# Expert gate and up weights in 1024-column pieces, and new PSUM banks for a task

## The reference

```
logits = (h @ w_router[i]).astype(F32)
top_v, top_i = lax.top_k(logits, TOP_K)                # TOP_K = 2 of N_EXP = 8
top_w = jax.nn.softmax(top_v, axis=-1)
for e in range(N_EXP):
    y = y + gates[..., e:e + 1] * swiglu(h, w_ex_gate[i, e], w_ex_up[i, e], w_ex_down[i, e])
# swiglu(h, wg, wu, wd) = (silu(h @ wg) * (h @ wu)) @ wd;  wg, wu: 1024 x 1408, wd: 1408 x 1024
```

## Time and profile before

| | us |
|---|---|
| median of 3 runs | 1520.3 |
| all runs | 1519.97, 1520.3, 1526.85 |
| span of the profiled execution (its time outside the span is not given) | 1521.1 |
| PE busy | 1484.1 |
| weight loads (PEld) busy | 1308.1 |
| DVE busy | 933.3 |
| ACT busy | 779.7 |

### The profile page before, as it was taken

The page is one execution under the profiler, slowest core; times in us unless marked ns, Lnnn a source line. Parts: engine busy times, 40 slices in busy tenths (PEclk is TensorE's granted clock), DMA queues, the critical chain, the costliest instruction groups (busy, mean ns, idle before and its releaser), DMA issues.

```text
span 1521.1 us, 22063 instructions
## 1 busy us (share of the span) xinstructions
PE 1484.1 (98%) x8722; PEld 1308.1 (86%) x8722; DVE 933.3 (61%) x1062; ACT 779.7 (51%) x889; POOL 53.7 (4%) x54
## 2 busy tenths in 40 slices
PE   7999999999999999999999999999999999999997
PEld 5788969699899999997889697998888888888875
DVE  4542265555554254346513655556998898988988
ACT  4443254543432242235333544535778778787875
POOL 0100000000000000001000000000000000000002
PEclk9999999999999999999999999999999999999999
DMA  9854265567752454265333554535999999999994
GB/s 327 269 171 160 97 222 166 167 213 234 259 161 93 149 135 121 91 221 171 122 118 111 167 167 139 167 115 184 332 369 392 381 381 374 377 389 380 374 383 160
DMA packets 236196, 342.50 MB, mean 225 GB/s; under 512 B 8661, under 2 KB 157054, under 8 KB 235854
## 3 DMA queue, kind: packets, MB, share of 16 engines
q1 hardware_dynamic: 227552, 313.32, 60.5%
q0 software_dynamic: 6496, 24.69, 4.4%
q10 hardware_dynamic: 2062, 3.24, 0.6%
HBM read 325.74 MB, written 15.47 MB: 224 GB/s over the span
## 4 chain that ended last, share of the span: by engine, by line
PE 90%; DVE 4%; DMA 2%; ACT 2%; SPq 1%; issue 1%; DVEq 0%; ACTq 0%
PE ps L701 26%; PE ps L703 26%; PE ps L702 25%; PE ps L718 2%; PE ps L943 2%; DMA raw<-in_w_ada_dram 1%; DVE wlo L2229 1%; PE ps L977 1%; SPq L476 1%; PE ps L961 1%; PE ps L728 1%; PE ps L1182 1%; DMA raw<-in_w_in_dram 1%; PE ps L799 1%; ACT whi L1647 1%
## 5 line engine op out<-in xcount | busy, mean ns | idle before, releaser
L701 PE MATMUL ps<-hhi,whi 128*128 128x384 f32 x824 | 276.6, 336 | 0.3 <-DVE hidlo L2326 0.3
L703 PE MATMUL ps<-hhi,wlo 128*128 128x384 f32 x824 | 275.3, 334 | 0.0
L702 PE MATMUL ps<-hlo,whi 128*128 128x384 f32 x824 | 275.3, 334 | 0.0
L1840 DVE TENSOR_TENSOR wlo<-raw,whi 128x2048 fp32r<-128x2048 f32 x65 | 148.7, 2289 | 179.2 <-ACT whi L1381 167.7
L2229 DVE TENSOR_TENSOR wlo<-raw,whi 128x2048 fp32r<-128x2048 f32 (+1 forms) x81 | 179.0, 2227 | 27.5 <-ACT whi L1647 26.9
L1647 ACT ACTIVATE whi<-raw 128x2048 fp32r<-128x2048 f32 (+1 forms) x81 | 150.5, 1868 | 49.9 <-PE ps L703 48.3
L2229 DVE TENSOR_TENSOR wlo<-mraw,whi 128x2048 fp32r<-128x2048 f32 (+2 forms) x81 | 160.7, 1992 | 14.8 <-ACT whi L1647 14.4
L701 PE MATMUL ps<-whi,xgh 128*128 128x512 f32 (+1 forms) x432 | 164.0, 380 | 3.5 <-DVE wlo L2229 2.0
L1647 ACT ACTIVATE whi<-mraw 128x2048 fp32r<-128x2048 f32 (+2 forms) x81 | 136.1, 1681 | 49.0 <-PE ps L703 48.9
L703 PE MATMUL ps<-whi,xgl 128*128 128x512 f32 (+1 forms) x432 | 160.9, 372 | 0.0
L702 PE MATMUL ps<-wlo,xgh 128*128 128x512 f32 (+1 forms) x432 | 160.5, 372 | 0.0
(11 more groups left out here) (352 smaller groups left out, 2495.3 us busy)
## 6 DMA issues: line engine op xcount, KB each, us to landing
raw<-in_w_ada_dram SPq DMA_DIRECT2D x62, 512.0 KB, 5.6
raw<-in_w_ex_up_dram SPq DMA_DIRECT2D x27, 1024.0 KB, 7.3
raw<-in_w_ex_down_dram SPq DMA_DIRECT2D x27, 1024.0 KB, 5.3
raw<-in_w_gate_dram SPq DMA_DIRECT2D x48, 512.0 KB, 4.6
raw<-in_w_in_dram SPq DMA_DIRECT2D x44, 512.0 KB, 6.0
raw<-in_w_ex_gate_dram SPq DMA_DIRECT2D x18, 1024.0 KB, 7.7
mraw<-in_w_ex_gate_dram SPq DMA_DIRECT2D x18, 1024.0 KB, 8.4
mraw<-in_w_ex_down_dram SPq DMA_DIRECT2D x18, 1024.0 KB, 8.8
```

Of the source, the lines that this page charges most:

```text
L701: pe.matmul(out, s[0], m[0], start=first, stop=False, **kw)
L702: pe.matmul(out, s[0], m[1], start=False, stop=False, **kw)
L703: return pe.matmul(out, s[1], m[0], start=False, stop=last, **kw)
L1840: dve.tensor_tensor(wlo[:, n % RING, :], raw[:, n % RING, :], whi[:, n % RING, :].bitcast(F32), ALU.subtract).then_inc(lo_done, 1)
```

## The change

A gate or up slot is now either wide, two channel tiles of 1024 columns (slots 0 to 3 gate, 4 to 7 up), or rest, four channel tiles of 384 columns (8 and 9 gate, 10 and 11 up). Slot sizes, their number and the six and three buffers stay. A wide slot's DMA reads runs of 4 KB, where all 512-column pieces had runs of 2 KB. One Silu and one product cover 1024 columns. The Silus stand in ACT's iterations 4 and 10, the products in DVE's 8 and 12, the turned products behind slots 8, 9 and 13, and `ehh` and `ehl` in iterations 9, 10 and 14. Banks: gate 0 and 1, up 2 and 3, rest 4 and 5, down output 6 and 7; turned products in 0, 1 and 4. `evalu` has memory of its own. The waits for `xg_ready` stand at slots 0 and 2 instead of 0 and 1.

```diff
-E_USED = [4 * CHUNKS[s // 4] for s in range(E_GU)] + [len(f) * D for f in E_DOWN]
+E_USED = [2 * WIDE] * (2 * E_WIDE) + [4 * CHUNKS[2]] * 4 + [len(f) * D for f in E_DOWN]
+TURNED = (0, 1, 4)
...
-                if s < E_GU:
-                    c, which, kh = s // 4, s % 4 // 2, s % 2
+                if s < 2 * E_WIDE:
+                    which, kp = divmod(s, E_WIDE)
+                    d = mraw[j][:, 0:E_USED[s]].rearrange("p (k c) -> p k c", k=2)
+                    src = w[which][:, 2 * kp:2 * kp + 2, 0:WIDE]
+                elif s < E_GU:
+                    which, kh = divmod(s - 2 * E_WIDE, 2)
                     d = mraw[j][:, 0:E_USED[s]].rearrange("p (k c) -> p k c", k=4)
-                    src = w[which][:, 4 * kh:4 * kh + 4, 512 * c:512 * c + CHUNKS[c]]
+                    src = w[which][:, 4 * kh:4 * kh + 4, WIDE:F_U]
...
-                    if s < 2:
-                        pe.wait_ge(xg_ready, 2 * q + s + 1)
+                    if s in (0, 2):
+                        pe.wait_ge(xg_ready, 2 * q + s // 2 + 1)
...
-                    if s % 4 == 0 and c != 1:
-                        pe.wait_ge(val_done, q * 3 + (3 if c == 0 else 4))
...
+                        for k in range(2):
+                            kk = 2 * kp + k
+                            for c in range(2):
+                                mm = mm3(ps[:, 2 * which + c, :], [y[:, kk, :] for y in (xgh, xgl)],
+                                         [y[:, k, 512 * c:512 * c + 512] for y in w], kk == 0, kk == KD - 1)
...
-                    if s in (5, 9):
-                        hidden_turned(s // 4 - 1, q)
+                    if s in (8, 9):
+                        hidden_turned(s - 8, q)
                     if s == 4 and more:
+                        pe.wait_ge(yv_ev, q + 1)
                         slots_of(q + 2)
...
+                        if more:
+                            pe.wait_ge(idx_ready, q + 1)
...
-                    if s in (2, 6, 10):
+                    if s == E_WIDE:
...
+                        act.activation(esil[:, :], ps[:, 0:2, :].rearrange("p a c -> p (a c)"), ACT.Silu).then_inc(esil_done, 1)
...
-                    if s in (4, 8, 12):
+                    if s == 2 * E_WIDE:
...
+                        dve.tensor_tensor(evalu[:, :], esil[:, :], ps[:, 2:4, :].rearrange("p a c -> p (a c)"), ALU.mult
+                                          ).then_inc(val_done, 1)
```

More of the change, by code:

```diff
@@ L270, in prefix_step_kernel @@
         assert rowx_at + 8 * BLK * N_EXP <= oraw_at
-        assert 5632 + 8 * KF * P <= 3 * 4 * 4 * T and 4 * SLOT * (MRAW - RING) + 12 * D <= top[0] - shared
+        assert 5632 + 8 * KF * P <= 3 * 4 * 4 * T and 4 * SLOT * (MRAW - RING) + 12 * D + 4 * WIDE <= top[0] - shared
         ssum = at("ssum", 2 * T, olo_at + 3072, shape=[2, T])
@@ L1177, in hidden_turned @@
             def hidden_turned(c, q):
-                pe.wait_ge(val_done, q * 3 + (c + 4))
-                pe.wait_ge(ehid_done, q * 3 + (c + 2))
+                pe.wait_ge(val_done, q * 2 + (4 if c == 2 else 3))
+                x = 512 * (c % 2)
                 for i in range(CHUNKS[c] // P):
-                    mm = pe.transpose(ps[:, 6 + c % 2, i * P:(i + 1) * P], evalu[:, i * P:(i + 1) * P], ident)
+                    mm = pe.transpose(ps[:, TURNED[c], i * P:(i + 1) * P], evalu[:, x + i * P:x + (i + 1) * P], ident)
                 mm.then_inc(ht_done, 1)
@@ L1187, in expert_task @@
                 for s in range(E_GU):
-                    c, which, kh = s // 4, s % 4 // 2, s % 2
-                    if s < 2:
-                        pe.wait_ge(xg_ready, 2 * q + s + 1)
+                    if s in (0, 2):
+                        pe.wait_ge(xg_ready, 2 * q + s // 2 + 1)
                     pe.wait_ge(lo_done, q * E_UNIT + split_count(n0 + s + 1))
-                    if s % 4 == 0 and c != 1:
-                        pe.wait_ge(val_done, q * 3 + (3 if c == 0 else 4))
[L1194 to L1198, removed]
+                    if s < 2 * E_WIDE:
+                        which, kp = divmod(s, E_WIDE)
+                        w = [x[:, s % RING, 0:E_USED[s]].rearrange("p (k c) -> p k c", k=2) for x in (whi, wlo)]
+                        for k in range(2):
[3 more added lines that the diff above has]
+                                         [y[:, k, 512 * c:512 * c + 512] for y in w], kk == 0, kk == KD - 1)
+                    else:
+                        which, kh = divmod(s - 2 * E_WIDE, 2)
+                        w = [x[:, s % RING, 0:E_USED[s]].rearrange("p (k c) -> p k c", k=4) for x in (whi, wlo)]
+                        for k in range(4):
+                            kk = 4 * kh + k
+                            mm = mm3(ps[:, 4 + which, 0:CHUNKS[2]], [y[:, kk, :] for y in (xgh, xgl)],
+                                     [y[:, k, :] for y in w], kk == 0, kk == KD - 1)
                     mm.then_inc(mm_done, 1)
-                    if s in (5, 9):
-                        hidden_turned(s // 4 - 1, q)
+                    if s in (8, 9):
+                        hidden_turned(s - 8, q)
                     if s == 4 and more:
+                        pe.wait_ge(yv_ev, q + 1)
                         slots_of(q + 2)
@@ L1214, in expert_task @@
                         for m in range(2):
-                            mm = mm3(ps[:, 4 + m, :], [y[:, kf, :] for y in (ehh, ehl)],
+                            mm = mm3(ps[:, 6 + m, :], [y[:, kf, :] for y in (ehh, ehl)],
                                      [y[:, c, m * 512:(m + 1) * 512] for y in w], kf == 0, kf == KF - 1)
@@ L1659, in expert_task @@
                         expert_hi(s + 2, q)
-                    if s in (2, 6, 10):
-                        c = s // 4
+                    if s == E_WIDE:
                         act.wait_ge(mm_done, q * E_UNIT + (n0 + s))
[L1663 to L1666, removed]
+                        act.wait_ge(val_done, q * 2 + 2)
+                        act.activation(esil[:, :], ps[:, 0:2, :].rearrange("p a c -> p (a c)"), ACT.Silu).then_inc(esil_done, 1)
+                    if s == 10:
+                        act.wait_ge(mm_done, q * E_UNIT + (n0 + s))
+                        act.wait_ge(val_done, q * 2 + 3)
+                        act.activation(esil[:, 0:CHUNKS[2]], ps[:, 4, 0:CHUNKS[2]], ACT.Silu).then_inc(esil_done, 1)
+                    if s in (9, 10, 14):
+                        c = min(s - 9, 2)
                         act.wait_ge(ht_done, q * 3 + (c + 1))
@@ L1670, in expert_task @@
                         act.activation(ehh[:, 4 * c:4 * c + CHUNKS[c] // P, :].rearrange("p k c -> p (k c)"),
-                                       ps[:, 6 + c % 2, 0:CHUNKS[c]], copy).then_inc(ehh_done, 1)
+                                       ps[:, TURNED[c], 0:CHUNKS[c]], copy).then_inc(ehh_done, 1)
                     if s == 13 and more:
@@ L1675, in expert_task @@
                         act.wait_ge(choice_tr, 1)
-                        act.activation(gat[:, :, :].rearrange("p b c -> p (b c)"), ps[:, 7, 0:T], copy).then_inc(choice_ready, 1)
+                        act.activation(gat[:, :, :].rearrange("p b c -> p (b c)"), ps[:, 5, 0:T], copy).then_inc(choice_ready, 1)
                         act.wait_ge(row_ready, 1)
@@ L1685, in expert_task @@
                 act.wait_ge(yd_out, q * 16 + 32)
-                act.activation(ysb[:, 0:512], ps[:, 4, :], copy).then_inc(ya_ev, 1)
+                act.activation(ysb[:, 0:512], ps[:, 6, :], copy).then_inc(ya_ev, 1)
             def experts():
@@ L2234, in expert_task @@
                 for s in range(E_UNIT):
[L2235 to L2236 removed]
+                    if s == 2 * E_WIDE:
                         dve.wait_ge(mm_done, q * E_UNIT + (n0 + s))
[L2238 to L2240 removed]
+                        dve.wait_ge(esil_done, q * 2 + 1)
+                        dve.tensor_tensor(evalu[:, :], esil[:, :], ps[:, 2:4, :].rearrange("p a c -> p (a c)"), ALU.mult
+                                          ).then_inc(val_done, 1)
+                    if s == E_GU:
+                        dve.wait_ge(mm_done, q * E_UNIT + (n0 + s))
+                        dve.wait_ge(esil_done, q * 2 + 2)
+                        dve.tensor_tensor(evalu[:, 0:CHUNKS[2]], esil[:, 0:CHUNKS[2]], ps[:, 5, 0:CHUNKS[2]], ALU.mult
+                                          ).then_inc(val_done, 1)
                     if more or s + 2 < E_UNIT:
                         expert_lo(s + 2, q)
[L2243 to L2244 removed]
+                    if s in (9, 10, 14):
+                        c = min(s - 9, 2)
                         dve.wait_ge(ehh_done, q * 3 + (c + 1))
                         k = slice(4 * c, 4 * c + CHUNKS[c] // P)
[L2247 removed]
+                        dve.tensor_tensor(ehl[:, k, :].rearrange("p k c -> p (k c)"), ps[:, TURNED[c], 0:CHUNKS[c]],
                                           ehh[:, k, :].rearrange("p k c -> p (k c)").bitcast(F32), ALU.subtract
@@ L2272, in expert_task @@
```

(2 more changed lines are left out.)

12 lines of the change are left out of this document (7 added, 5 removed).

## The result

In twenty runs each, the changed kernel took 1527.87 us in the median and the kernel before 1523.02; the ratio, which is reckoned from all runs and not from the two medians (they lie 4.9 us apart), is 1.0025, 95% interval 1.0016 to 1.0033. That is slower by 3.8 us (2.4 to 5.0) and under the 0.5% that was called no change. The forecast was +2.5 us. Its 1522.8 us in absolute terms stood on a median of three runs, which lay 2.7 us under that of twenty; put on these three by the ratio, the changed kernel takes 1524.1 us, within the range of 1519 to 1527, while the 1527.87 us as they stand lie 0.9 above it. One run of a later version took 2101.04 us at a granted clock of 0.653, and it is left out of every comparison.

The account below looks back on a forecast made before the run. TensorE was taken to set the pace, DVE next, loads hidden. Slot 7's 2.0 us plus the last task's 0.5 gave 2.5 us on a 1521.1 us span: 1523.6 of span, 1522.8 us timed, range 1519 to 1527.

Parts of the forecast that it names:

- The stop at slot 7: Loop tasks: late Silu with its table load delays slot 7's split, PE loses 0.25 us a task, 2.0 in eight.
- the walk: Slot-by-slot reckoning of ACT, DVE and PE times in a task; it put PE's slot 7 start at 1231.19.
- The last task: Ninth expert task: wide product and transposes push slot 12 from 1486.87 to 1487.4, 0.5 us, bounds -0.3 and 1.2.
- The product and the transposes: Loop tasks, DVE iterations 8 to 10: product ready with 0.3 us margin, value 0, bounds 0 and 1.2 a task.
- Rival C: Transposes behind slot 8 stop PE for a late product, up to 1.2 us in nine tasks, about 1531; chance 0.08.
- The loads: Expert weight DMAs: eight of twelve get 4 KB runs, all land early enough, value 0.
- B: Loads are the clock, so larger runs would take away 6.5 us of PE's losses, 1513.8; chance 0.05.
- The sign named for them: Expert stage: loads of wide slots land sooner, with no effect.
- The table load's price: On ACT before the Silu: 1.28 us from the trace, without the skill's extra drain of about 1.38 us.
- D: Table load holds ACT 2.7 us, slot 7's wait grows to 1.6 us, 13 us in eight tasks, 1533.8; chance 0.02.
- A: Walk 0.2 us too pessimistic at slot 7, PE never stops, only the last task's term stays, 1520.8; chance 0.20.
- the base: Starting time for the forecast: profiled span 1521.1 us, timed median 1520.3, 0.8 below the span.

Follow-up runs that it names:

- the last pair of kernels: Changed kernel and kernel before, both with short down slot second, later gathered-rows split and last-task DVE reorder, the changed one also with early table load: 0.9964 and 0.9962.
- the longer Silu: Changed kernel with an extra 1.0 us copy pass on ACT directly before the wide Silu in all nine tasks: ratio 1.0053.
- the two kernels with halves: Changed kernel with Silu and product by 512 columns: 0.9994; the same plus table load at the pass head, short down slot second, last-task reorder: 0.9999.
- the right set: Changed kernel with table load in ACT's iteration 2, last-task DVE reorder, short down slot second and gathered-rows split in iteration 15: ratio 0.9964.

## Why the prediction was right

**The stop at slot 7** was the first term, 2.0 us in eight tasks. On the clock of the earlier trace rows the walk had PE start at 1231.19; put on the changed kernel's task, which starts 2.0 us earlier, it started at 1231.13. Measured: the eight tasks are 1.7 us longer in all, and the stop stands in each of them in both profiles, 0.11 to 0.23 us. The table load moved early takes it away, and the tasks then fall by 2.2 us, 0.5 below the kernel before; the prediction had put the rest of the layout at 0. Half a Silu less takes it away too, and 0.92 us more on ACT adds 0.91 a task. Shown, from both sides.

**The last task** was put at 0.5 us and took 0.27 in the profile, within its bounds. The walk had the wide product at 25.4 us into the task; it came at 25.0, and slot 12 followed at 33.6, 0.3 us sooner than reckoned. What was not priced is that a stop of over 2 us could be followed by a fall of the clock, 1.6 us more, in the second profile. So the 2.5 us are borne out by the 2.0 us of the stage. The 3.8 us of the timing hold about 1 us of lower clock besides, for which the prediction had no term; that they too lie near the forecast is in part luck.

**The product and the transposes** cost nothing in the loop tasks, as walked: no stop behind slot 8, in eight of eight. Rival C falls there. Its mechanism, PE held by a late product, is seen only in the last task, where the forecast had it.

**The loads** cost and gained nothing in time, so the value of 0 holds, and B falls. The sign named for them came too: wide slots land sooner with no effect, 7.6 us against 8.1 over the stage. But the reading behind it was thin: the 5.6 us of the earlier trace rows are three down loads, while over the stage the down slots' mean is 7.8 us, hardly under the 8.1 of the 2 KB slots. The Trainium skill (DMA: Bandwidth & Descriptors, Why small descriptors are slow) speaks for longer runs; an estimate by its figures is 2%, 0.2 us of such a landing. The trace agrees in the direction and shows more, 0.5 us, and 1.7 us in the last pair of kernels.

**The table load's price** was taken from the trace at 1.28 us and holds: the Silu starts 0.01 us behind it again. D falls: where the longer Silu held ACT up by 0.92 us, the tasks grew by 0.91, and no such growth is there.

**A** said no stop at slot 7, and one came in eight of eight tasks.

**What failed is the base**: "so 1523.6 of span and 1522.8 us timed". I took the timed median to be 0.8 us below the span. The runs that are listed with their spans take 2.2 to 2.3 us more than these (2.5 to 2.6 in the two kernels with halves), so the profiled execution of before took about 1523.3, an estimate, and the three first runs were on average faster than it (1522.4). From that base the forecast would have been 1525.8, still 2 us under the 1527.87 measured, where the lower clock comes in.

## What to carry to other kernels

An engine with 20% of idle time can still have none at one place of a ring: count the chain (free buffer, split, split, start) against the slots that cover it, slot by slot, and look at what an edit moves into the chain that has no room. A merge of two operations that saves 0.3 us of engine time cost 0.2 a task, because it put a 1.28 us table load into a place where nothing hid it; one dummy operation moved it back. And compare the clocks of the runs before a difference in time is given to the edit. Remove the last stops together: a mend alone gained at most 0.3 us a task, as the next stop stood close behind, and the right set gained 0.7.

## What the runs showed of the hardware

TensorE's granted clock fell from 2.4 to 1.2 GHz for some 3 us at a time, or twice that, both in stretches of nearly full work and behind stops. Table by stretch of the second profile of the changed kernel, in full work ahead of the expert stage:

```profile
678.20:688.20 10.00, 10.00 (x71) 10.00 (x69) 8.42 (x18) 5.24 (x7) 0.00 (x0) 1.00 0.29 101
688.20:695.00 6.80, 6.80 (x53) 4.14 (x56) 2.06 (x6) 1.02 (x3) 0.00 (x0) 0.50 0.49 157
```

and behind the stop of its last task:

```profile
1484.00:1486.00 2.00, 0.42 (x3) 0.10 (x1) 1.65 (x7) 1.48 (x1) 0.56 (x1) 1.00 0.89 324
1486.00:1488.00 2.00, 1.56 (x8) 1.56 (x9) 2.00 (x3) 0.60 (x1) 1.70 (x2) 0.74 1.02 418
1488.00:1490.00 2.00, 2.00 (x8) 2.00 (x7) 2.00 (x3) 0.00 (x0) 1.70 (x2) 0.50 1.02 418
1490.00:1492.00 2.00, 2.00 (x13) 1.96 (x13) 1.10 (x4) 1.22 (x1) 1.47 (x2) 0.91 1.03 418
```

PE was busy for 0.42 of 2 us, then the clock stood at 0.74, 0.50 and 0.91, and the task took 1.57 us longer than its twin. In the profiles whose last task has a stop of 2 us or more such a fall followed it in three of six; in the eight others, whose longest stop there is 1.7 us or less, in none. A stop near 210 us goes the same way: of 1.96 to 2.75 us it was followed by a fall in five profiles of five, of 1.42 to 1.73 us in one of five. But one of 1.45 us near 32 us was followed by a fall in five of nine, so its length does not decide alone. That a stop brings the fall is likely by these counts and not shown. Falls ahead of the expert stage, in parts that no edit touched, go with its start: at half clock for 3.4 us in all it starts at 1062.9 us, for 13.7 at 1066.6 and for 23.9 at 1071.5. Runs of one kernel differ by up to 10 us here, and in those of the kernel before the mean granted clock accounts for about two thirds of the variance.
